# Hybrid diffusion trunk, one core: two more weight slabs of the input projection as pairs of seven half-sized products

## What is computed

```python
h = _rmsnorm(xl, norm_mix[l]) * (1.0 + ml[1]) + ml[0]
aq, ak, av, bq, bk, bv, cq, ck, cv, cg, gates = _split_projection(h, w_in[l])   # z = h @ w_in
aq = _axial_rope(aq, n_lat)
ak = _axial_rope(ak, n_lat)
a_o = _diff_output(_diff_attention(aq, k_all, v_all, lam), diff_norm[l], lam_init)
b_o = _neighbourhood_attention(bq, bk, bv, cache_b_k, cache_b_v, na_rpb[l])     # context tokens: plain softmax
c_raw, _, _ = _bidirectional_retention(cq, ck, cv, log_gamma, s0_fwd, s0_bwd)
```

## Time and profile before

| | |
|---|---|
| median of 3 runs | 1903.09 us (1903.05 to 1903.37) |
| the profiled execution | 1902.24 us, of which its span is 1900.4 us |
| granted TensorE clock, mean | 0.999 of full speed (2.4 GHz) |
| TensorE (PE) busy | 94% of the span |
| VectorE (DVE), ScalarE (ACT), GpSimd (POOL) busy | 34%, 20%, 17% |
| ahead, A and B of layer 0 | 40 to 277 us of the span |
| ahead, A and B of layer 1 | 970 to 1210 us |

### The profile page before, as it was taken

One profiled execution on the slowest core, in us unless ns is written; L12 is line 12 of the kernel. 1 busy time (PEld: TensorE's weight loads), 2 busy tenths in 40 slices (PEclk: granted clock), 3 DMA queues, 4 the chain that ended last, 5 costly groups with the idle time before them and its releaser, 6 DMA issues.

```text
span 1900.4 us, 22341 instructions
## 1 busy us (share of the span) xinstructions
PE 1778.6 (94%) x9266; PEld 1051.7 (55%) x9266; DVE 652.6 (34%) x1328; ACT 376.9 (20%) x853; POOL 330.3 (17%) x193
## 2 busy tenths in 40 slices
PE   6999999999999988788799999999999998888887
PEld 3595567999634333233266755689995343333323
DVE  2853354565311211111158434445643111111103
ACT  3223334001301010010132242330112110101002
POOL 2520006953100000000035100275610000000000
PEclk9999999999999999999999999999999999999999
DMA  9525152425999999999992244214378999999996
GB/s 389 200 92 222 67 222 78 178 89 217 359 413 427 427 428 428 427 429 428 410 387 100 89 183 177 100 46 177 134 299 331 428 428 428 427 428 427 428 428 271
DMA packets 54853, 553.19 MB, mean 291 GB/s; under 512 B 5984, under 2 KB 9952, under 8 KB 13280
## 3 DMA queue, kind: packets, MB, share of 16 engines
q1 hardware_dynamic: 50976, 549.13, 69.8%
q10 hardware_dynamic: 3776, 2.62, 0.4%
HBM read 547.54 MB, written 4.19 MB: 290 GB/s over the span
## 4 chain that ended last, share of the span: by engine, by line
PE 68%; DMA 29%; DVE 1%; issue 1%; ACT 0%; SPq 0%; DVEq 0%; ACTq 0%
PE psum L1373 17%; PE psum L1600 14%; DMA ring<-in_w_up 8%; DMA dense<-in_w_down 8%; DMA ring<-in_w_gate 8%; PE psum L1122 8%; PE psum L1124 7%; PE psum L1131 4%; DMA dense<-in_w_gate 4%; PE psum L470 2%; PE psum L1081 2%; PE psum L1292 2%; PE psum L1212 1%; PE psum L1570 1%; PE psum L1468 1%; PE psum L1102 1%
## 5 line engine op out<-in xcount | busy, mean ns | idle before, releaser
L1600 PE MATMUL psum<-ring,dense 128*64 128x512 f32 x960 | 216.2, 596 | 31.6 <-DMA ring<-in_w_gate 17.8
L1600 PE MATMUL psum<-dense 128*64 128x512 f32 x704 | 158.7, 595 | 23.7 <-DMA dense<-in_w_gate 16.8
L1600 PEld LDWEIGHTS psum<-ring,dense 128*64 128x64 f32 x960 | 68.5, 137 | 170.4 <-issue 139.3
L858 POOL TENSOR_TENSOR tmp<-square 128x384 f32<-128x384 f32 x5 | 5.0, 1000 | 855.1 <-ACT square L1732 855.1
L1122 PE MATMUL psum<-hT,ring 128*128 128x384 f32 x464 | 153.4, 488 | 0.0
L2465 DVE TENSOR_TENSOR state<-state,psum 128x512 f32<-128x512 f32 x32 | 22.0, 687 | 372.8 <-PE psum L1600 334.8
L1124 PE MATMUL psum<-ring,hT 128*128 128x512 f32 x288 | 126.5, 594 | 0.0
L1122 PEld LDWEIGHTS psum<-hT,ring 128*128 128x128 f32 x464 | 87.5, 190 | 60.8 <-issue 1.4
L1600 PEld LDWEIGHTS psum<-dense 128*64 128x64 f32 x704 | 49.2, 137 | 129.3 <-issue 95.0
L2040 ACT ACTIVATE kcT<-psum 32x512 f32<-32x512 f32 x60 | 35.2, 587 | 423.8 <-PE psum L1600 423.4
L2502 DVE COPY decays<-psum 16x512 f32<-16x512 f32 x60 | 41.4, 689 | 220.4 <-PE psum L1600 220.0
(11 more groups left out here) (327 smaller groups left out, 2733.0 us busy)
## 6 DMA issues: line engine op xcount, KB each, us to landing
dense<-in_w_gate SPq DMA_DIRECT2D x34, 2048.0 KB, 35.8
ring<-in_w_in SPq DMA_DIRECT2D x60, 1024.0 KB, 10.5
ring<-in_w_up SPq DMA_DIRECT2D x30, 2048.0 KB, 37.6
ring<-in_w_gate SPq DMA_DIRECT2D x30, 2048.0 KB, 36.2
wide<-in_w_up SPq DMA_DIRECT2D x22, 2048.0 KB, 38.3
dense<-in_w_down SPq DMA_DIRECT2D x20, 2048.0 KB, 40.3
ring<-in_w_mod SPq DMA_DIRECT2D x38, 1024.0 KB, 8.9
ring<-in_w_down SPq DMA_DIRECT2D x18, 2048.0 KB, 40.1
```

The source lines that it names most:

```text
L1600: last = M.matmul(psum[HALF * half:HALF * (half + 1), bank, :], lhsT(k), SPARE_BLOCKS[2 * kk + half] if spare else w[:, kk, half * SLAB:(h ...
```

## The change

Slabs 1 (AK) and 6 (CQ, CK) become pairs too, so there are 8 pairs a layer instead of 4: pairs 0, 1 of slab 1, then 2, 3 of slab 3, 4, 5 of slab 4 and 6, 7 of slab 6. Pairs 0 and 1 run ahead of the attentions, between groups 9 and 10; pairs 2 to 7 fill steps 0 to 11 of A. Groups 19 to 21 (second attention's values) move to the end of A and the start of B, and modulation slabs move to later steps. DVE does the last four rotations after the sums of the pair that makes their chunks. POOL makes the weight sums of pairs 2 and 3 before the bias additions, cuts these into eight operations of 128x512, and starts them (and the sums of pair 3) only after all rotations. `ck` is scaled by two ScalarE operations in B.

```diff
-FIRST_PAIRED, LAST_PAIRED = 3, 4
-Z_PAIRS = [(slab, p) for slab in (FIRST_PAIRED, LAST_PAIRED) for p in range(2)]
+PAIRED = {1: 12, 3: 4, 4: 16, 6: 20}
+Z_PAIRS = [(slab, p) for slab in PAIRED for p in range(2)]
+PAIRS_AHEAD = 2
...
-        Z_FIRST = 11
+        Z_AHEAD = [0, 1, 2, 3, 8, 9, 10]
...
         def a_fill(l):
 
             m = DENSE_MODS[l]
-            return [[("pair", l, i), ("half", l, i)][h:h + 1] for i in range(len(Z_PAIRS)) for h in range(2)] + [[("z", l, 19 + t)] for t in range(3)] + [
-                [("mod", l, m[0]), ("mod", l, m[1])], [("modT", l, m[0]), ("mod", l, m[2])], [("modT", l, m[1]), ("modT", l, m[2])]]
+            steps = [[("pair", l, i), ("half", l, i)][h:h + 1] for i in range(PAIRS_AHEAD, len(Z_PAIRS)) for h in range(2)]
+            return steps + [[("mod", l, m[0]), ("mod", l, m[1])], [("modT", l, m[0]), ("modT", l, m[1]), ("z", l, 19)]]
 
         def b_fill(l):
 
             m = DENSE_MODS[l]
-            steps = [[("norm", l, t), ("z", l, 22 + t)] for t in range(4)] + [[("z", l, 26)], [("z", l, 27)]]
-            steps += [[("z", l, 28), ("mod", l, m[3]), ("mod", l, m[4])], [("z", l, 29)], [("z", l, 30)], [("modT", l, m[3]), ("mod", l, m[5])],
-                      [("z", l, 31)], [("z", l, 32)]]
+            steps = [[("norm", l, t), ("z", l, g)] for t, g in enumerate((20, 21, 26, 27))]
+            steps += [[("z", l, 28)], [("mod", l, m[2]), ("mod", l, m[3])], [("modT", l, m[2]), ("z", l, 29)], [("modT", l, m[3]), ("z", l, 30)],
+                      [("z", l, 31)], [("mod", l, m[4]), ("mod", l, m[5])], [("modT", l, m[4]), ("z", l, 32)]]
             if len(m) == 7:
-                return steps + [[("modT", l, m[4]), ("mod", l, m[6])], [("modT", l, m[5]), ("modT", l, m[6])]]
-            return steps + [[("modT", l, m[4])], [("modT", l, m[5])]]
+                return steps + [[("modT", l, m[5]), ("mod", l, m[6])], [("modT", l, m[6])], []]
+            return steps + [[("modT", l, m[5])], [], []]
...
                     G.tensor_tensor(in_decay[:], in_decay[:], bwd_decay[:], ALU.add).then_inc(in_decay_ready, 1)
+                    z_pair_weight_sums(2)
+                    pool.wait_ge(rope_done, at(rope_done, 8))
+                    z_pair_weight_sums(3)
                     pool.wait_ge(bias_in, at(bias_in, 32))
                     for b in bias:
-                        rows = b.rearrange("p h (r c) -> p (h r) c", c=GRID_W)
-                        G.tensor_tensor(rows, rows, c_("window").unsqueeze(1).to_broadcast([P, 32, GRID_W]), ALU.add).then_inc(bias_ready, 1)
-                    z_pair_weight_sums(2)
-                    z_pair_weight_sums(3)
+                        for part in range(4):
+                            rows = b.rearrange("p h (r c) -> p (h r) c", c=GRID_W)[:, 8 * part:8 * (part + 1)]
+                            G.tensor_tensor(rows, rows, c_("window").unsqueeze(1).to_broadcast([P, 8, GRID_W]), ALU.add).then_inc(bias_ready, 1)
+                    for i in range(4, len(Z_PAIRS) - 1):
+                        z_pair_weight_sums(i)
...
-                    for g in range(Z_FIRST):
+                    for g in Z_AHEAD[0:-1]:
                         z_group(layer, g)
+                    for i in range(PAIRS_AHEAD):
+                        z_pair(layer, i)
+                        z_half(layer, i)
+                    z_group(layer, Z_AHEAD[-1])
                     pe.wait_ge(keys_in, at(keys_in, 16))
                     pe.wait_ge(rope_done, at(rope_done, 8))
...
+                    for c in range(4):
+                        rotate(c)
+                    for i in range(PAIRS_AHEAD):
+                        z_begin_sums(i)
+                        z_end_sums(i)
+                        dve.wait_ge(z_pair_summed, at(z_pair_summed, 4 * i + 4))
+                        rotate(4 + 2 * i)
+                        rotate(5 + 2 * i)
                     for n in range(UNITS):
                         row_max(n)
                         normalise(n)
-                        if n < 2 * len(Z_PAIRS):
-                            (z_begin_sums, z_end_sums)[n % 2](n // 2)
+                        (z_begin_sums, z_end_sums)[n % 2](PAIRS_AHEAD + n // 2)
```

More of the change, by code:

```diff
@@ L187, in build @@
         AQ, BQ, CG, AK, BK, CQ, CK = 0, 4, 8, 12, 16, 20, 22
-        ROTATED = [AQ + c for c in range(4)] + [AK + c for c in range(4)]
+        ROTATED = [AQ + c for c in range(4)] + [AK + c for c in (0, 2, 1, 3)]
         v_rows = dense[:, 24 * T:24 * T + 9 * SLAB].rearrange("p (m b e) -> p m b e", m=3, b=NBLK)
@@ L291, in z_pair_banks @@
         def z_pair_banks(i):
-            a, b, c = [Z_PAIR_BANKS[(i + n) % 3] for n in range(3)]
+            banks = S + TR[1:] if i < PAIRS_AHEAD else Z_PAIR_BANKS
+            a, b, c = [banks[(i + n) % 3] for n in range(3)]
             return a, b, c, a
@@ L525, in build @@
         CHAIN_FILL = [chain_fill(l) for l in range(DEPTH)]
-        FILL = [x for l in range(DEPTH) for x in START_FILL[l] + [("z", l, g) for g in range(Z_FIRST)]
+        FILL = [x for l in range(DEPTH) for x in START_FILL[l] + [("z", l, g) for g in Z_AHEAD]
                 + [y for step in A_FILL[l] + B_FILL[l] for y in step if y[0] not in ("pair", "half")] + CHAIN_FILL[l]]
@@ L677, in wait_slab_free @@
                 eng.wait_ge(z_full, f_of("mod", l, j) + 1)
-            elif kind == "w_in" and j in (FIRST_PAIRED, LAST_PAIRED):
+            elif kind == "w_in" and j in PAIRED:
                 eng.wait_ge(z_pair_full, at(z_pair_full, 7 * (Z_PAIRS.index((j, 1)) + 1)))
@@ L891, in z_pair_weight_sums @@
                         w = [[z_weight_quarter(layer, slab, p, kh, nh) for nh in range(2)] for kh in range(2)]
[L892 removed]
+                        sums = Z_WEIGHT_SUMS[i]
                         z_sum(sums[0], w[0][1], w[0][0], ALU.subtract)
@@ L1136, in z_weights @@
                         slab, p = Z_PAIRS[i]
-                        return [[z_weight_quarter(layer, slab, p, kh, nh) for nh in range(2)] for kh in range(2)], Z_WEIGHT_SUMS[p]
+                        return [[z_weight_quarter(layer, slab, p, kh, nh) for nh in range(2)] for kh in range(2)], Z_WEIGHT_SUMS[i]
                     def z_pair(l, i):
@@ L2138, in decays, with rotate @@
                         dve.wait_ge(decay_ready, at(decay_ready, 1))
-                    for c in range(8):
+                    def rotate(c):
                         if c == 2:
                             decays()
-                        dve.wait_ge(z_read, f_of("z", layer, c) + 1)
+                        if c < 4:
+                            dve.wait_ge(z_read, f_of("z", layer, c) + 1)
                         if c >= 2:
@@ L2192, in z_outer @@
                         slab, p = Z_PAIRS[i]
-                        first = ({3: BQ, 4: BK}[slab] + p) * T
+                        first = (PAIRED[slab] + p) * T
                         return dense[:, first:first + 10 * TOKENS].rearrange("p (s t) -> p s t", s=2)[:, :, 0:TOKENS]
@@ L2198, in z_inner @@
                         slab, p = Z_PAIRS[i]
-                        first = ({3: BQ, 4: BK}[slab] + p) * T + TOKENS
+                        first = (PAIRED[slab] + p) * T + TOKENS
                         return dense[:, first:first + 6 * TOKENS].rearrange("p (s t) -> p s t", s=2)[:, :, 0:TOKENS]
```

55 lines of the change are left out of this document (35 added, 20 removed).

## The result

The changed kernel takes 1916.94 us (median of 4 runs, 1915.22 to 1921.61) beside 1903.07 us for the kernel before in the same session: ratio 1.0076, 95% interval 1.0064 to 1.0088. The direction was forecast, the size was not: +13.9 us where +5.9 us stood, and outside the range. The profiled execution took 1917.06 us with a span of 1915.2 us, 14.8 us more than before, and the mean granted clock is 0.994 in place of 0.999.

The account below looks back on a forecast made before the run. TensorE, busy 94% of the span, was taken as the bound. Layer 0: -1.6 - 2.2 + 4.5 (A's stalls) + 1.3 = +2.0 us; layer 1, with 3.2 last, +3.9; together +5.9, 1909.0 us, range 1899.0 to 1912.5.

Parts of the forecast that it names:

- Ahead: Before the attentions: pairs 0 and 1 save 2.4 us, a longer wait takes back 0.8; -1.6 us a layer.
- Rival 3: Ahead of the attentions: rotations also ready in time, POOL not holding the fifth; -5.7 us, 1897.4; chance 0.09.
- Slab 6's products: Within the attentions: two pairs (18.8 us) replace four groups (21.0 us); -2.2 us a layer.
- A, unit 1: In A: DVE's chain, held by POOL, takes 7.5 us against TensorE's 5.1 us of work; stall 2.4 us.
- Rival 2: In A: POOL's moved work costs nothing, the chains slip through; -3.1 us, 1900.0; chance 0.12.
- rival 1: In A: only one of two units stalls, or L2184 is free; +1.4 to +1.9 us, about 1904.7; chance 0.17.
- A, unit 2: In A: DVE arrives late and held, 8.4 us against TensorE's 6.3 us of work; stall 2.1 us.
- The end of B: Behind B's last scores: a 4.9 us chain loses group 32's cover; stalls of 1.3 us (layer 0), 3.2 us (layer 1).
- Nothing in the two steps behind it is short by more than 0.1 us: At B's end: the two steps behind lack at most 0.1 us of cover.
- A shift of the attentions passes to the end one to one: From the attentions through the experts' stage: any shift reaches the kernel's end at full size.
- Rival 5: Layer 0's first gate: slab 9 lands after some 14 us, not 7; +5 us, 1914; chance 0.05.
- Rival 4: In A: larger stalls, 6 us a layer; +8.9 us, 1912.0; chance 0.12.

Follow-up runs that it names:

- tail_and_gaps: tail_covered with POOL's eight bias additions moved: four ahead of pair 2's sums, three after unit 3's row maximum, one after unit 6's; 1897.51 us.
- no_additions: The changed kernel with POOL's eight bias additions covering only one row in eight each; 1911.52 us.
- additions_in_unit1_of_before: The kernel before, with bias additions cut in eight and held back until DVE has unit 0's row maximum; 1910.76 us.
- idle_filled_to_size: The changed kernel with unread products sized to fill four idle times of TensorE, including one in the retention; 1911.92 us.
- pool_late: The changed kernel, with POOL's first gate sums also waiting until DVE has finished the modulation rows; 1912.0 us.
- bare_tail_in_before: The kernel before, with slab 8's last group moved ahead of B's last scores in layer 1 alone; 1914.89 us.
- tail_covered: The changed kernel with B's fill at its end in the old pattern, row-groups of slab 8 behind the last two scores; 1905.4 us.
- idle_filled: The changed kernel with unread products in three idle times of TensorE, none in the retention; they overran the stalls; 1917.51 us.

## Why the prediction was right in sign and wrong in size

- **Ahead, -1.6 us a layer: right.** -1.66 us in layer 0, with the wait of 1.31 us before the first scores that it named (1.3). Rival 3 (POOL does not hold the fifth rotation) falls with it: that rotation took 6.2 us in place of 2.7.
- **Slab 6's products, -2.2 us a layer: nearly.** 2.5 us, by tail_and_gaps.
- **A, unit 1, 2.4 us: right,** 2.49 and 2.51 us, for the reason given: no_additions takes the wait away, and additions_in_unit1_of_before makes it without any pair. Rival 2 (POOL costs A nothing) is refuted, and so is rival 1's free L2184: its counterpart stood 1.39 us.
- **A, unit 2, 2.1 us: mis-sized,** 0.90 us where the clock was whole. POOL's run ended sooner than the 21 us it was given (90.55 to 110.92 us in layer 0), so only the two short operations of this unit's chain were held (1.11 and 0.95 us), and the two long ones ran free (0.42 and 0.62 us). In layer 0 unit 1's half clock hid the wait.
- **"The end of B", 1.3 and 3.2 us: mis-sized,** 1.84 and 3.69 us, half a microsecond short in both. The chain itself was right: from the last scores (270.68) to the end of the last normalising operation (275.58) it takes 4.9 us, as forecast. But the transposes also wait until DVE has copied the previous unit's transposes out of PSUM (`pT_dve` in `probs_transposed`), and this copy stands behind the chain on DVE. Before, group 32 covered it. DVE in the changed kernel, layer 0:

```profile
275.17 0.41 DVE L2216 TENSOR_SCALAR wide<-wide,small 128x384 f32<-128x384 f32 x1
275.50 0.55 DVE L2289 COPY wide<-psum 128x384 f32<-128x384 f32 x1
```

- **"Nothing in the two steps behind it is short by more than 0.1 us"** holds for these steps, but the moved slabs and groups, costed "at nothing", made small waits elsewhere: 0.38 us before the first modulation slab, 0.68 in place of 0.28 at a norm, 0.29 in step 6 of B, 1.1 us a layer.
- **The missing term: TensorE's clock, which the sum left out.** It priced each stall at its length. Behind unit 1 of layer 0 the half clock cost 1.7 us (4.45 in place of 2.77), behind B's end in layer 1 2.3 us (from 1213.06 to gate(0) 5.40 us; idle_filled_to_size needs 3.1 us for the same rows at the whole clock), in the retention 2.4 us (from 1233.30 to the next gate 5.5 us, before 3.0). Together 6.4 us, more than the whole forecast (5.5 us net of the wait of unit 2 that it hid).
- **"A shift of the attentions passes to the end one to one": the step that failed.** It held in layer 0 (2.78 us in, 2.71 out). In layer 1 the shift changed which operations meet: TensorE's work slid, the slab loads did not, the store between them landed in 2.0 in place of 4.5 us, and POOL's first gate sum fell on DVE's two small operations. 3.2 us of new wait, and behind it the 2.4 us of half clock named above, 5.6 of the 8.9 us that the forecast fell short. pool_late takes the wait away alone, and the bare tail makes it without any of the new pairs (bare_tail_in_before).

Added up: 5.9 forecast, + 6.4 (clock) + 3.2 (collision) + 2.2 (small waits) + 1.0 (B's end) + 0.2 (unit 1) - 3.3 (unit 2) - 0.6 (slab 6) - 0.2 (ahead) = 14.8 us, the difference of the spans. The exact agreement is partly luck: by these terms the attention stretches of the two layers come out 0.2 us longer each than in the table, and the 0.4 us behind gate(1) are in none of them.

Rival 5 (slab 9 late, 1914) had the nearest time and did not occur: gate(0) of layer 0 follows its transposes without a wait. Rival 4, "larger stalls" in A (1912.0), had the wrong reason too: the stalls of A were 2.5 and 3.4 us in the two layers, below the 4.5 of the forecast; what stood behind the stalls made them dear.

## What to carry to other kernels

A stall on an engine that is otherwise never idle is priced at its length plus what the clock takes after it; here stalls of 1.8 to 4 us cost up to 2.4 us more each, and sometimes nothing (the tail alone, 3.7 us long, took 11.5 us in all). A shift can be taken to pass on one to one only where nothing behind it is paced by transfers (here layer 0 passed it on and layer 1 did not): look at each engine that starts on a transfer's landing and ask what it would meet. And work for the shared GpSimd is placed by what runs beside it at that time, small blocks first, not by what it follows in the program: tail_and_gaps has the same instructions on POOL as the changed kernel and is 19.4 us faster with them and B's end moved.

## What was not expected of the hardware

- The clock's answer to the same wait differs. Behind a wait of 2.39 to 2.51 us in unit 1 the next 16 products (2.77 us at the whole clock) took 4.45 and 2.77 us in the two layers of the changed kernel, 4.45 and 3.60 in tail_covered, 4.24 and 4.45 in pool_late. Behind the 1.84 us at the end of B in layer 0 it halved in no_additions and not in the changed kernel. Behind the 3.6 to 4.0 us in the retention it halved in the changed kernel, in idle_filled and in no_additions, and not in bare_tail_in_before. What decides it was not tried. The spread may come from it, which was not tested: the four runs of the changed kernel lie 6.4 us apart, with mean clocks of 0.993 in the slowest and 0.995 in the fastest; the six of tail_and_gaps, at 0.998 and 0.999, lie 1.2 us apart.
- Unread products in the idle time make the kernel 5 us faster.
- An operation of 0.17 us on 16 elements stood 1.83 us, since it is held for the whole of POOL's operation however small it is itself.
